# Differential attention in a fused two-block kernel: the tile norm spread over three items, one mixing step per item, the score scale moved into the queries

## The reference

```python
def diff_attn_block(qb, keys, vals, lam):
    s = jnp.einsum('bqhmd,bkhmd->bhmqk', qb, keys).astype(jnp.float32) * (DIFF_HEAD_DIM ** -0.5)
    p = jax.nn.softmax(s, axis=-1)
    a = p[:, :, 0] - lam * p[:, :, 1]
    return jnp.einsum('bhqk,bkhv->bqhv', a.astype(vals.dtype), vals)

def diff_post(o, subln_g, lam_init):
    B, L = o.shape[:2]
    return (rms_norm_2(o, subln_g) * (1 - lam_init)).reshape(B, L, DIFF_V_WIDTH)
```

## Time and profile before

| what | value |
|---|---|
| median of 3 runs | 2147.21 us (2138.06 to 2158.22) |
| the profiled execution's own time | 2141.53 us |
| its span in the trace | 2139.7 us |
| TensorE busy, share of the span | 1864.0 us, 87% |
| VectorE busy | 843.9 us, 39% |
| ScalarE busy | 503.1 us, 24% |
| mean granted TensorE clock | 0.919 of full speed |

### The profile page before, as it was taken

The page is one execution under the profiler, slowest core; times in us unless marked ns, Lnnn a source line. Parts: engine busy times, 40 slices in busy tenths (PEclk is TensorE's granted clock), DMA queues, the critical chain, the costliest instruction groups (busy, mean ns, idle before and its releaser), DMA issues.

```text
span 2139.7 us, 29839 instructions
## 1 busy us (share of the span) xinstructions
PE 1864.0 (87%) x12850; PEld 974.0 (46%) x12850; DVE 843.9 (39%) x1432; ACT 503.1 (24%) x928; POOL 100.4 (5%) x139
## 2 busy tenths in 40 slices
PE   5999798889998789988999999999996988877874
PEld 2444233343544545545666676764453333333331
DVE  3031535363645736434454445443454221121112
ACT  3100355331114621234333333212111000000000
POOL 0000000000000000020000000000001000000001
PEclk8999667999999889989899999999996999999997
DMA  8112433424111020031112111125736999999997
GB/s 358 56 63 79 157 123 121 195 111 178 52 40 40 1 91 23 0 119 55 46 61 61 51 54 62 33 96 211 290 141 265 427 426 427 426 426 427 427 426 274
DMA packets 51700, 370.11 MB, mean 173 GB/s; under 512 B 8241, under 2 KB 8385, under 8 KB 33003
## 3 DMA queue, kind: packets, MB, share of 16 engines
q1 hardware_dynamic: 38651, 319.95, 37.4%
q0 software_dynamic: 12912, 48.19, 6.1%
HBM read 344.99 MB, written 31.51 MB: 176 GB/s over the span
## 4 chain that ended last, share of the span: by engine, by line
PE 40%; DMA 13%; DVE 7%; ACT 2%; issue 1%; SPq 0%; DVEq 0%; POOLq 0%; ACTq 0%
PE psum L203 39%; DMA arena<-in_w 13%; DVE arena L150 3%; ACT arena L200 2%; DVE arena L160 1%; PE psum L206 1%; DVE arena L168 1%; DVE arena L155 1%; DVE arena L180 1%; DMA arena<-yd 0%; DVE arena L188 0%; DVE arena L184 0%; DVE arena L164 0%; DMA arena<-fd,arena 0%; ACT L200 0%
## 5 line engine op out<-in xcount | busy, mean ns | idle before, releaser
L203 PE MATMUL psum<-arena 64*64 64x32 f32 (+10 forms) x12202 | 1777.2, 368 | 219.7 <-DMA arena<-in_w 71.2
L203 PEld LDWEIGHTS psum<-arena 64*64 64x64 f32 (+4 forms) x12202 | 897.4, 154 | 1041.8 <-issue 871.4
L200 ACT ACTIVATE arena<-psum 128x512 f32<-128x512 f32 (+7 forms) x357 | 186.8, 523 | 1189.2 <-PE psum L203 1020.3
L150 DVE TENSOR_TENSOR arena<-arena,psum 128x512 f32<-128x512 f32 (+3 forms) x140 | 76.4, 546 | 493.8 <-ACT arena L200 246.7
L150 DVE TENSOR_TENSOR arena<-arena 128x512 f32<-128x512 f32 (+12 forms) x316 | 191.7, 607 | 39.4 <-ACT arena L200 9.3
L150 DVE TENSOR_TENSOR arena<-psum,arena 128x256 f32<-128x256 f32 (+2 forms) x146 | 80.2, 549 | 319.6 <-PE psum L203 315.0
L200 ACT ACTIVATE arena<-arena 128x128 f32<-128x128 f32 (+10 forms) x242 | 134.8, 557 | 262.1 <-DVE arena L150 90.0
L160 DVE SCALAR_TENSOR_TENSOR arena<-arena 128x512 f32<-128x512 f32 (+6 forms) x142 | 110.9, 781 | 49.7 <-ACT arena L200 45.0
L206 PE MATMUL psum<-arena 128*128 128x128 f32 x648 | 104.8, 301 | 29.0 <-DVE arena L160 22.9
L206 PEld LDWEIGHTS psum<-arena 128*128 128x128 f32 x648 | 78.6, 153 | 96.0 <-issue 49.1
L200 ACT ACTIVATE arena<-psum,arena 128x128 f32<-128x128 f32 (+3 forms) x157 | 82.3, 524 | 158.0 <-PE psum L203 119.7
(11 more groups left out here) (46 smaller groups left out, 149.8 us busy)
## 6 DMA issues: line engine op xcount, KB each, us to landing
arena<-in_w SPq DMA_DIRECT2D x131, 2048.0 KB, 32.5
arena<-in_w SPq DMA_DIRECT2D x48, 256.0 KB, 2.9
arena<-kd POOLq DMA_DIRECT2D x28, 256.0 KB, 3.9
gd<-arena SPq DMA_DIRECT2D x24, 256.0 KB, 3.0
arena<-gd SPq DMA_DIRECT2D x24, 256.0 KB, 8.3
arena<-in_w POOLq DMA_DIRECT2D x2, 2048.0 KB, 9.3
fd<-arena POOLq DMA_DIRECT2D x8, 512.0 KB, 3.9
arena<-in_w SPq DMA_DIRECT2D x4, 1024.0 KB, 26.8
```

The source lines that it names most:

```text
L150: return self.ends(self.e.tensor_tensor(out, a, b, op))
L200: return self.ends(self.e.activation(out, a, func, **kw))
L203: return self.ends(self.e.matmul(out, lhs, rhs, start=start, stop=stop))
```

## The change

Five things change, all in the differential attention but one.

The score scale moves into the queries: the vector `qn`, by which the queries are multiplied in `proj2`, is itself multiplied by 0.125 once, and the exponential loses `scale=0.125`. The row maximum is written negated by the reduce itself, so the multiplication by -0.125 after each reduce goes.

The mixing step no longer divides by the first map's row sum. With row sums s0 and s1 it forms p1 * (s0 * lambda / s1) - p0, which is -s0 times what was formed before. The sign goes into a final factor of -LAM1, and since the norm after it divides by the root mean square, s0 falls out there, except for the 1e-6, which is multiplied by s0 squared. The sums s0 of a tile's four heads are kept in `st2[:, 44:52]` for that.

The norm of a tile is spread: copy and squares stay in iteration 4i + 6, two new VectorE operations on 128 x 4 (`yv`) come in iteration 4i + 7, ScalarE's root comes at the end of its iteration 4i + 7 (written there as x - 4), VectorE's reciprocal and two multiplications come in iteration 4i + 8, TensorE's four transposes in iteration 4i + 9 after the values' matmuls, and VectorE's copy of them in iteration 4i + 10.

```diff
                 if (n, m) == ("pool", 3):
+                    V.ts(P["qn"], P["qn"], 0.125, None, ALU.mult)
...
+        sum0 = lambda i, h: st2[:, 44 + 4 * (i % 2) + h:45 + 4 * (i % 2) + h]
...
-                if x % 4 == 0 and x >= 8:
-                    out((x - 8) // 4)
...
                     T.then_inc("pv2", x - 3)
+                if x % 4 == 1 and x >= 9:
+                    out((x - 9) // 4)
...
-            for x in range(NX + 3):
+            for x in range(NX + 4):
                 if x < NX:
-                    o = 4 * (x % 2)
+                    o, i = 4 * (x % 2), IT2[x][0]
                     for mp in range(2):
+                        total = (sum0(*IT2[x]), st2[:, 8 + o:9 + o])[mp]
                         A.wait_ge(V["m2", x, mp])
                         if x > 2:
                             A.wait_ge(T["pt2", x - 3])
+                        if IT2[x][1] == 0 and i > 1:
+                            A.wait_ge(V["yv", i - 2])
                         A.act(Pm[x % 3][mp], ps["s2", x, mp][:, 0:768], ACT.Exp, bias=st2[:, o + mp:o + mp + 1],
-                              scale=0.125, accum_out=st2[:, 8 + o + mp:9 + o + mp]).then_inc("e2", x, mp)
+                              accum_out=total).then_inc("e2", x, mp)
...
-                        A.wait_ge(V["yd", i - 1])
+                        A.wait_ge(V["yv", i - 1])
...
-                    A.act(st2[:, 36:40], st2[:, 32:36], ACT.Sqrt, bias=eps[:, 0:1], scale=1.0 / 128).then_inc("yd", i)
+                    A.mark("y2", i)
+                if 0 <= x - 4 < NX and IT2[x - 4][1] == 3:
+                    i = IT2[x - 4][0]
+                    A.wait_ge(V["yv", i])
+                    if i > 0:
+                        A.wait_ge(V["yd", i - 1])
+                    A.act(st2[:, 36:40], st2[:, 52:56], ACT.Sqrt, scale=1.0 / 128).then_inc("yd", i)
...
-                        V.red(s, ps["s2", x, mp][:, 0:768], ALU.max)
-                        V.ts(s, s, -0.125, None, ALU.mult).then_inc("m2", x, mp)
+                        V.red(st2[:, o + mp:o + mp + 1], ps["s2", x, mp][:, 0:768], ALU.max, negate=True).then_inc("m2", x, mp)
...
-                    V.rec(rc, st2[:, 8 + o:10 + o])
-                    V.tt(rc[:, 1:2], rc[:, 1:2], lamc, ALU.mult)
-                    V.ts(p[1], p[1], rc[:, 1:2], None, ALU.mult)
-                    V.stt(p[0], p[0], rc[:, 0:1], p[1], ALU.mult, ALU.subtract).then_inc("mix2", x - 1)
-                if x % 4 == 0 and x >= 8:
-                    out((x - 8) // 4)
-                if 0 <= x - 3 < NX and IT2[x - 3][1] == 3:
-                    i = IT2[x - 3][0]
+                    V.rec(rc, st2[:, 8 + o:9 + o])
+                    V.stt(rc, sum0(*IT2[x - 1]), lamc, rc, ALU.mult, ALU.mult)
+                    V.stt(p[0], p[1], rc, p[0], ALU.mult, ALU.subtract).then_inc("mix2", x - 1)
+                if 0 <= x - 4 < NX and IT2[x - 4][1] == 3:
+                    i = IT2[x - 4][0]
+                    s4 = st2[:, 44 + 4 * (i % 2):48 + 4 * (i % 2)]
+                    V.wait_ge(A["y2", i])
+                    V.tt(s4, s4, s4, ALU.mult)
+                    V.stt(st2[:, 52:56], s4, 128.0 * EPS, st2[:, 32:36], ALU.mult, ALU.add).then_inc("yv", i)
+                if 0 <= x - 5 < NX and IT2[x - 5][1] == 3:
+                    i = IT2[x - 5][0]
...
-                    V.stt(y, y, LAM1, SUB, ALU.mult, ALU.mult).then_inc("yd", i)
+                    V.stt(y, y, -LAM1, SUB, ALU.mult, ALU.mult).then_inc("yd", i)
+                if x % 4 == 2 and x >= 10:
+                    out((x - 10) // 4)
```

More of the change, by code:

```diff
@@ L1403, in out @@
                 ps.free(V.last(), "tb", i)
-            for x in range(NX + 3):
+            for x in range(NX + 5):
                 if x < NX:
@@ L1408, in diff_vector @@
                     for mp in range(2):
-                        s = st2[:, o + mp:o + mp + 1]
                         V.wait_ge(T["s2", x, mp])
@@ L1412, in diff_vector @@
                             V.wait_ge(A["e2", x - 2, mp])
-                        V.red(s, ps["s2", x, mp][:, 0:768], ALU.max)
-                        V.ts(s, s, -0.125, None, ALU.mult).then_inc("m2", x, mp)
+                        V.red(st2[:, o + mp:o + mp + 1], ps["s2", x, mp][:, 0:768], ALU.max, negate=True).then_inc("m2", x, mp)
                 if 0 <= x - 1 < NX:
                     o, p = 4 * ((x - 1) % 2), Pm[(x - 1) % 3]
-                    rc = st2[:, 16 + o:18 + o]
+                    rc = st2[:, 16 + o:17 + o]
                     V.wait_ge(A["e2", x - 1, 1])
-                    V.rec(rc, st2[:, 8 + o:10 + o])
-                    V.tt(rc[:, 1:2], rc[:, 1:2], lamc, ALU.mult)
-                    V.ts(p[1], p[1], rc[:, 1:2], None, ALU.mult)
-                    V.stt(p[0], p[0], rc[:, 0:1], p[1], ALU.mult, ALU.subtract).then_inc("mix2", x - 1)
-                if x % 4 == 0 and x >= 8:
-                    out((x - 8) // 4)
-                if 0 <= x - 3 < NX and IT2[x - 3][1] == 3:
-                    i = IT2[x - 3][0]
+                    V.rec(rc, st2[:, 8 + o:9 + o])
[9 more added lines that the diff above has]
+                    i = IT2[x - 5][0]
                     y = ATN[i % 2]
```

## The result

The changed kernel takes 2128.99 us (median of 9 runs, 2121.93 to 2139.72) against 2146.58 us for the kernel before (9 runs, 2138.06 to 2159.45). The ratio is 0.9916 with a 95% interval of 0.9892 to 0.9940, so about 18 us less, between 13 and 23. The forecast was 22.5 us less, 2125.

A forecast was written before the change was run, and what follows sets the result against it. VectorE bounds an item and ScalarE's root a norm, on the chain to TensorE. Start 8.7, tiles 5.0 and 6.4, tail 2.4 sum to 22.5 us off 2147.2, so 2124.7, say 2125; range 2109 to 2142.

The forecast's parts named there:

- VectorE's item, and what is late next: Attention items: VectorE's work falls 1.0 us to 3.66, but items come 4.17 us apart, gaining 0.50 each.
- loop: Scores, maximum, exponentials, transposes and products across both maps: 4.71 plus 3.63 gives 8.34 us for two items, 4.17 each.
- The start: Items 0 to 7 of the attention stage: item 7's first maximum at 686.6 instead of 695.32, 8.7 us earlier.
- A norm, spread: Tiles between items 7 and 15: 20.8 then 20.05 us against 25.75 and 26.50, gaining 5.0 and 6.4.
- rival B: TensorE's clock still falls at every norm, costing 2 to 3 us a tile; gain 14 to 16, time 2132; chance 0.20.
- The tail: Item 15's maximum to the stage's last transposes: 16.3 us instead of 18.67, 2.4 less.
- The sum: Whole kernel: 8.7 + 5.0 + 6.4 + 2.4 = 22.5 us saved, forecast 2125.
- The two bounds stated beside the sum: Tile limits: 17.4 us from engine work, 30 us gained in all; 22.0 with ScalarE's 5.3 us exposed, 17 gained.
- rival C: Attention items stay at 4.67 us and only the norms gain: 12 us plus 4 at the start, 2133; chance 0.10.
- The signs: Stage checks: exponentials of items 7 and 8 late by 1 to 2 us; no reciprocal wait over 1 us but the last.
- D: The stage's gain is lost waiting at the program end's expert-weight stream; same time, 2145; chance 0.06.
- E: TensorE's clock stays at half through the whole stage, making the kernel 18 us slower, 2166; chance 0.03.

The follow-up runs named there:

- spread_only: The kernel before with only the norm spread over three items, mixing, maxima and scale as before; 2125.5 us, ratio 0.9916 to the kernel before.
- items_only: The kernel before with only the cheaper item (scale in queries, negated maximum, one mixing pass), norm where it stood; 2141.6 us, ratio 0.9981.
- negate_back: The changed kernel with each maximum's negation put back as a small VectorE operation behind the reduce, twice an item; 2130.7 us in one run.
- newton_root: The changed kernel with the norm's root moved from ScalarE to VectorE by two Newton steps, no table loads; 2131.2 us, ratio 0.9944.
- newton_split: The changed kernel with the root on VectorE by Newton steps, the norm's work in three pieces, one copy on ScalarE; 2131.9 us, ratio 0.9926.

## Why the prediction was right, and where it was off

The view that decided was that an item is VectorE's and a norm is ScalarE's latency. spread_only and items_only show each alone, at 95.8 and 105.8 us where the same steps gave 95 and 106.6, against 113.1 before.

*VectorE's item, and what is late next.* Predicted 3.66 us of work and a loop of 4.17. Measured 4.17, with 0.24 and 0.92 us of waiting in turn. Two items share the loop's two parts, 4.71 and 3.63; how the 8.34 us divide between the two items (4.52 and 3.83 in one profile, 4.64 and 3.72 in the other) was not forecast. negate_back lengthened one part and gave 4.36, as the same sum does. The small scalar_tensor_tensor and the negating reduce cost what was taken (the pair with the large one 1.27, two reduces 2.02).

*The start.* Item 7's first maximum came 33.52 us after item 0's scores began, against 42.18 before: 8.7 us earlier, as predicted.

*A norm, spread.* Predicted 20.05 us a tile in step. Items 11 to 15 took 20.2. Items 7 to 11 took 22.4 where 20.8 was predicted, and this is the one term of the stage that was mis-sized (3.4 us gained in place of 5.0; the other terms came out at 8.7, 6.3 and 2.3 for 8.7, 6.4 and 2.4): the first of the tiles holds the 3.4 us at half clock, with item 10 6.74 us behind item 9. That is rival B in one tile of three, at 1.6 us, where it was priced at 2 to 3 us in each of them. That it came in one only is luck as far as the runs show: the waits are the same in the next tile, and no step of the prediction says which of them the clock follows. Both profiles of the changed kernel have it in the same place.

*The tail.* Predicted 16.3 us from item 15's maximum to the last transposes; measured 751.53 - 735.17 = 16.36.

*The sum.* 22.5 predicted, 20.6 in the stage, 18 (13 to 23) in the times. The first difference is the low clock in tile 1. The second is inside the interval. The two profiles differ by more than that outside the stage, 5.9 us ahead of it and 3.9 behind. The length ahead changes between runs of one kernel (659.0 and 665.6 in the changed one, 652.8 and 659.2 in spread_only); the 3.9 us behind are all in the stretch of the recurrent stage and came again. The forecast took the code behind the stage as unchanged, and that is not borne out to this size. The two bounds stated beside the sum don't add up: with its own terms for start and tail, tiles of 17.4 us give 28.6 and tiles of 22.0 us give 19.4, not 30 and 17; and rival C's 16 us give 2131, not 2133. Neither moves the forecast.

*The signs.* Two came out a little beyond what was written: item 8's exponential was 2.3 us late (1 to 2), and the reciprocal of tile 2 waited 1.01 us.

*The rivals.* C fell: items became shorter. D fell in its form: what was lost behind the stage stands ahead of the stream of expert weights, in the recurrent stage, where the DMA share is 0.20. E fell: the stage's mean clock rose, as its rows before and after show.

```profile
653.10:766.20 113.10, 84.54 (x428) 60.31 (x428) 75.38 (x143) 64.98 (x128) 0.00 (x0) 0.84 0.05 19
```

```profile
659.00:751.50 92.50, 76.55 (x428) 55.28 (x428) 62.72 (x103) 62.08 (x126) 0.00 (x0) 0.91 0.06 24
```

The rule of the Trainium skill on a table switch (ScalarE: Activation LUTs, "What ACT_TABLE_LOAD costs") did not show its drain here either: the loads at 698.27 and 699.85 are each followed within 0.02 us by the next operation. The first load starts 0.07 us after the copy before it ends. The advice of the same page of the Trainium skill (section "Table sets: the hidden batching unit"), to do all exponentials and then all roots, pointed at something real all the same: item 8's exponential waited for both loads. Without them a tile at full clock took 19.3 us in newton_root and 19.0 in newton_split, where it was 20.2, so they are worth about 1 us a tile.

## What to carry to other kernels

When one engine waits for another's result at the same place in every round, move the use of the result a round or two later in the queue before making any operation cheaper: here that gave 17.3 of the 20.6 us, and the cheaper operations alone gave 7.3. After such a move look at how long the moved work keeps the next round waiting: here 3.0 us in one block in front of the next maxima cost 0.3 us a tile more than the same work in pieces, as long as the clock held. The larger difference, 4.3 us, stood in a tile in which the clock fell, and that a block brings this on is not shown. To price a cheaper operation, write down the loop that an item runs through and see whether the operation is on it; 0.65 us off the loop cost 0.13 an item, and 0.5 us that stood on it cost 0.19.

## What the runs showed of the hardware that I had not expected

TensorE's clock falls in code that no one touched, and not at the same place in each execution. Ahead of the stage, one stretch with the same 127 matmuls and 31 operations of VectorE, in the kernel before and in the changed one:

```profile
290.50:334.20 43.70, 36.42 (x127) 13.95 (x125) 20.44 (x31) 26.50 (x48) 1.51 (x3) 0.72 0.36 137
```

```profile
292.70:342.00 49.30, 48.09 (x127) 17.24 (x125) 20.42 (x31) 27.68 (x50) 1.51 (x3) 0.52 0.32 122
```

From the operation of VectorE that begins it to the copy that follows it, the stretch takes 43.7 us in one profile and 49.4 in the other, with the clock at 0.72 and 0.52. Over all twelve profiles the code ahead of the stage took between 647.1 and 666.1 us and the code behind it between 1373.5 and 1386.5, a spread as large as the change's whole effect. Ahead of the stage this is scatter, and a kernel's second profile can differ by 9 us from its first; behind it the kernel has a part in it, as said above. A single profile's span would have put the gain at 10.8 us, against 18 from the medians and 20.6 in the stage: the effect of such a change is read in the stage, and its worth in the time only from many runs.

A short wait can bring the clock down and a longer one need not. In the changed kernel 1.14 us before item 9 was followed by 3.4 us at half clock, and the same wait of 1.14 us a tile later by none; in newton_root 1.43 us was followed by 6.8 us, and 1.42 us a tile later by none.
